# Gates table of a product-key layer: first keys made by GpSimd with their weights, state split moved one stage earlier

## The chip, the core and the metric

The kernel runs on one core of one Trainium2 chip. The core has five engines with queues of their own: TensorE (PE in the profile; PEld is its weight load), VectorE (DVE), ScalarE (ACT), GpSimd (POOL) and SyncE (SP, which here only starts transfers). The metric is the device time of one execution in microseconds, less is better. The median of three runs before the change is 2322.55 us.

## What is computed

The reference is one step of a streaming encoder layer for 512 prompt tokens and 8 x 16 sample tokens (640 tokens, 1024 features): stick-breaking and latent attention, then a product-key layer. Only the latter matters here. For each token, 8 heads choose 16 of 128 x 128 experts each:

```python
q = (x @ w_peer_q).reshape(n, PEER_HEADS, 2, PEER_HALF)
s1 = jnp.einsum('nhk,ek->nhe', q[:, :, 0], sub_keys_1)
s2 = jnp.einsum('nhk,ek->nhe', q[:, :, 1], sub_keys_2)
...
gate = jax.nn.softmax(top_s, axis=-1)
...
act = jax.nn.gelu(jnp.einsum('td,thkd->thk', xt, u), approximate=False) * gt
return jnp.einsum('thk,thkd->td', act, v_experts[it])
```

So a token's result is a sum over its 128 chosen experts (8 heads x 16) of gate x gelu(token . u) x v. The expert's number is first key x 128 + second key.

## The kernel before, in words

The kernel is written by hand as eight phases, one after the other, each a block of one instruction queue per engine that ends with a barrier of all engines; semaphores order the work inside a block. The 640 tokens are five tiles of 128. The first two tiles (GT = 2) get their experts by gathering rows from memory; the other three (DN = 384 tokens, "dense") run against all 16,384 experts, with a table of gates that is zero where an expert was not chosen. The last three phases matter.

**phase_keys** (line 1583) makes queries and scores on TensorE, ScalarE copies them out of PSUM (queries at L1664, scores at L1676), and VectorE finds the 16 best per head (MAX8, FIND_INDEX8 and MATCH_REPLACE8, which read one tensor). After a tile's maxima VectorE casts the indices (L1777), adds candidates (L1780 to L1784), finds the best pairs, and compares (L1812). GpSimd then multiplies and adds up these comparisons for tiles 0 to 3 (L1637, L1641, L1650), VectorE those of tile 4 (L1815 on). The results for the dense tokens are transposed into `sel`: for every dense token, a column of 128 first keys, 128 second keys and 128 gates, one per partition.

**phase_gates** (line 1868) builds the table of gates. For each token, `first` holds on each of 128 partitions (one per head and choice) a row of 128 zeros with the gate at the chosen first key, `second` a row with a one at the chosen second key; TensorE multiplies the two and so sums the 128 choices into a 128 x 128 table. The work goes in groups of G = 4 tokens, 96 groups in all, with four buffers of `first` and `second` and four PSUM banks in turn. Before the change VectorE makes the first keys of three tokens in one comparison without weights (L1949), those of the fourth with the weight in one tensor_scalar of two operations (L1953), and all four second keys (L1954). ScalarE multiplies the three unweighted ones by their gates (`weigh`, L1990) and copies a finished bank into `stage` (L1997). TensorE waits for `hot_ready` (VectorE), `weighed` (ScalarE) and a free bank (`table_ready`), and signals `hot_used`, for which VectorE waits four groups later. SP stores every 64 tokens of the table to memory (L1927, the last ones in four parts, L1931). GpSimd has other work at the start: it splits the dense tokens' normed state `hT` into a rounded upper part `h[0]` (cast, L1936) and the rest `h[1]` (subtraction, L1938), which the experts phase multiplies by; then it issues the first three gathers of expert rows (AHEAD = 3, L1864, in `gather`). SP loads the first `vraw` tiles after the split, since they lie over `hT`.

**phase_experts** (line 2004) runs 128 chunks of 128 experts: TensorE transposes `u` (L2189), multiplies in split precision (L2200, L2212); ScalarE and VectorE copy and split (L2124, L2239, L2163, L2290); GpSimd multiplies by the gates (L2117) and issues the gathers; VectorE works on the gathered rows (L2249, L2263).

Of the kernel before, what the change touches and what calls it, by code (L numbers as in the profile page):

```python
# [25 lines left out]
F32R = mybir.dt.float32r  # L26
ALU = mybir.AluOpType
ACT = mybir.ActivationFunctionType
# [3 lines left out]
P = 128  # L32
D = 1024
KD = D // P
# [5 lines left out]
N = SEQ + NSEQ * STEP  # L40
NT = N // P
PT = SEQ // P
HALF = N // 2
GT = 2
DT = NT - GT
DN = DT * P
# [11 lines left out]
NKEYS = 128  # L58
TOPK = 16
NEXP = NKEYS * NKEYS  # L60
NQ = 2 * H
# [11 lines left out]
HI, LO = 0, 1  # L73
# [719 lines left out]
def phase_prompt_attention(nc, A, env):  # L793
# [19 lines left out]
             "mT_psum aT_psum mT0 mT1 aT0 aT1 om_psum os_psum om_out os_out").split()  # L813
    S = {n: sem("pa_" + n) for n in names}
    ROUNDS = [(i, hp) for i in range(PT) for hp in range(H // 2)]
# [767 lines left out]
def phase_keys(nc, A, env):  # L1583

    sb, sem, PS, C, ident = (env[k] for k in ("sb", "sem", "PS", "C", "ident"))
    hT = env["hT"]
# [20 lines left out]
    sel = sb("sel", 10, [P, 3, DN])  # L1607
    eidx = sb("eidx", 14.5, [P, GT, H * TOPK], U32)
    egate = sb("egate", 15.5, [P, GT, H * TOPK])
    htok = sb("htok", 122, [P, GT, D])  # L1610
# [2 lines left out]
    place, work = sb("place", 148, [P, H * TOPK]), sb("work", 148.5, [P, 2, H * TOPK])  # L1613
    flat_stat = env["stat"][:].rearrange("p a b -> p (a b)")
    total, peak = flat_stat[:, 0:NT * H], flat_stat[:, 64:64 + H]
    env["env"].update(sel=sel, eidx=eidx, egate=egate, htok=htok)
    names = "sk_psum sk_ready q_ready s_psum s_ready topped ranked gate_exp gates sel_psum sel_ready0 sel_ready1 h_psum h_turned hot_ready hot_used picking picked step".split()
    S = {n: sem("pk_" + n) for n in names}
    S["q_psum"] = env["q_psum"]
    skey_raw = env["skey_raw"]  # L1620
# [1 line left out]
    with nc.Block() as block:  # L1622
# [4 lines left out]
        @block.gpsimd  # L1627
        def _(pool):
            step = Step(pool, S["picking"])

            def sync(ins):
                step(ins)
                step.wait()

            for t in range(NT - 1):
                pool.wait_ge(S["hot_ready"], t + 1)
                sync(pool.tensor_tensor(hot[:], hot[:], topf[t % 2][:].unsqueeze(3).broadcast_to((P, NQ, TOPK, TOPK)), ALU.mult))  # L1637
                src = hot
                for half in halves:
                    w = half.shape[2]  # L1640
                    ins = pool.tensor_tensor(half[:], src[:, :, 0:w, :], src[:, :, w:2 * w, :], ALU.add)  # L1641
                    if src is hot:
                        ins.then_inc(S["hot_used"], 1)
                        pool.wait_ge(S["hot_used"], t + 1)
                    else:
                        sync(ins)
                    src = half
                pairs = src[:].rearrange("p (h i) m k -> p h i m k", i=2)
                for i in range(2):
                    ins = pool.tensor_tensor(pick[:, t, i, :].rearrange("p (h k) -> p h k", h=H), pairs[:, :, i, 0, :], pairs[:, :, i, 1, :], ALU.add)  # L1650
                    if i == 0:
                        step(ins)
                ins.then_inc(S["picked"], 1)

        @block.scalar
        def _(act):
# [211 lines left out]
def phase_gates(nc, A, env):  # L1868

    sb, sem, PS, C, sel = (env[k] for k in ("sb", "sem", "PS", "C", "sel"))  # L1870
    hT = env["hT"]
    stage = [sb(f"stage{i}", 138 + 32 * i, [P, NKEYS, TB]) for i in range(2)]
    G = 4
    first = [sb(f"first{i}", 66 + 2 * i, [P, G, NKEYS]) for i in range(G)]
    second = [sb(f"second{i}", 74 + 2 * i, [P, G, NKEYS]) for i in range(G)]

    h = [sb("h_hi", 82, [P, KD, DN], F32R), sb("h_lo", 94, [P, KD, DN], F32R)]
    dense = hT[:, :, GT * P:N]
    u = [sb(f"u{i}", 106 + 4 * i, [P, D]) for i in range(4)]
    vraw = [sb(f"vraw{i}", 46 + 4 * i, [P, D]) for i in range(2)]  # L1880
    rows = [sb(f"rows{i}", at, [P, D]) for i, at in enumerate((54, 58, 62, 10, 203, 176, 180, 184, 188, 192, 196))]
    v_in = [nc.alloc_semaphore(f"v_in{i}") for i in range(2)]
    row_in = [nc.alloc_semaphore(f"row_in{i}") for i in range(len(rows))]
    parts = [nc.alloc_semaphore(f"gates_part{i}") for i in range(PARTS)]
    steps = gather_order()
    eidx = env["eidx"]
    env["env"].update(h=h, u=u, vraw=vraw, rows=rows, v_in=v_in, row_in=row_in, steps=steps, gates_parts=parts)
    h_split, u_in = sem("gt_h_split"), sem("gt_u_in")
    S = {n: sem("gt_" + n) for n in "marked hot_ready weighed hot_used table_ready".split()}

    stored = [nc.alloc_semaphore(f"gates_stored{i}") for i in range(2)]
    env["env"].update(gates_stored=stored)
# [24 lines left out]
    with nc.Block() as block:  # L1917
        @block.sync
        def _(sp):
            for i in range(len(u)):  # L1920
                sp.dma_start(u[i][:], A["u_experts"][0, i * P:(i + 1) * P, :]).then_inc(u_in, 16)
            sp.wait_ge(h_split, 2)
            for i in range(2):
                sp.dma_start(vraw[i][:], A["v_experts"][0, i * P:(i + 1) * P, :]).then_inc(v_in[i], 16)
            for b in range(BLOCKS - 1):
                sp.wait_ge(S["table_ready"], (b + 1) * PB + G)
                sp.dma_start(A["gates"][b], stage[b % 2][:]).then_inc(stored[b % 2], 16)  # L1927
            sp.wait_ge(S["table_ready"], BLOCKS * PB + G)
            for i in range(PARTS):
                keys = slice(i * NKEYS // PARTS, (i + 1) * NKEYS // PARTS)  # L1930
                sp.dma_start(A["gates"][BLOCKS - 1, :, keys, :], stage[1][:, keys, :]).then_inc(parts[i], 16)  # L1931
            sp.wait_ge(u_in, 16 * len(u))

        @block.gpsimd
        def _(pool):
            pool.tensor_copy(h[0][:], dense).then_inc(h_split, 1)  # L1936
            pool.wait_ge(h_split, 1)
            pool.tensor_tensor(h[1][:], dense, h[0][:], ALU.subtract).then_inc(h_split, 1)  # L1938
            pool.wait_ge(h_split, 2)
            for n in range(AHEAD):  # L1940
                gather(pool, A, eidx, steps, rows, row_in, n)

        @block.vector
        def _(dve):
            def body(n, g, e, at, token, last):

                dve.wait_ge(S["hot_used"], n + 1)

                dve.tensor_tensor(first[g][:, 0:G - 1, :], C["iota"].unsqueeze(1).broadcast_to((P, G - 1, NKEYS)),  # L1949
                                  sel[:, 0, bass.ds(token, G - 1)].unsqueeze(2).broadcast_to((P, G - 1, NKEYS)), ALU.is_equal  # L1950
                                  ).then_inc(S["marked"], 1)
                col = bass.ds(token + (G - 1), 1)
                dve.tensor_scalar(first[g][:, G - 1, :], C["iota"], sel[:, 0, col], sel[:, 2, col], ALU.is_equal, ALU.mult)  # L1953
                dve.tensor_tensor(second[g][:], C["iota"].unsqueeze(1).broadcast_to((P, G, NKEYS)),  # L1954
                                  sel[:, 1, bass.ds(token, G)].unsqueeze(2).broadcast_to((P, G, NKEYS)), ALU.is_equal
                                  ).then_inc(S["hot_ready"], 1)

            loop(dve, body)

        @block.tensor  # L1960
        def _(pe):

            pe.sem_inc(S["hot_used"], G)

            def body(n, g, e, at, token, last):
                pe.wait_ge(S["hot_ready"], n + 1)
                pe.wait_ge(S["weighed"], n + 1)
                pe.wait_ge(S["table_ready"], n + 1)
                for j in range(G):
                    mm = pe.matmul(PS[:, g, j * NKEYS:(j + 1) * NKEYS], second[g][:, j, :], first[g][:, j, :], start=True, stop=True)  # L1970
                mm.then_inc(S["hot_used"], 1)

            loop(pe, body)

        @block.scalar
        def _(act):

            act.sem_inc(S["table_ready"], G)
            for e in range(2):
                act.sem_inc(stored[e], 16)  # L1980

            def edge(pair, e):

                act.wait_ge(stored[e], pair * 16 + 16)

            def weigh(n, g, token):

                act.wait_ge(S["marked"], n + 1)
                for j in range(G - 1):
                    ins = act.activation(first[g][:, j, :], first[g][:, j, :], ACT.Copy, scale=sel[:, 2, bass.ds(token + j, 1)])  # L1990
                ins.then_inc(S["weighed"], 1)

            def body(n, g, e, at, token, last):
                if not last:
                    weigh(n + 1, (g + 1) % G, token + G)
                act.wait_ge(S["hot_used"], n + G + 1)
                act.activation(stage[e][:, :, bass.ds(at, G)], PS[:, g, :].rearrange("p (n i) -> p i n", n=G),  # L1997
                               ACT.Copy).then_inc(S["table_ready"], 1)

            weigh(0, 0, 0)  # L2000
            loop(act, body, edge)


# [334 lines left out]
```

## Time and profile before

| | before |
|---|---|
| median of 3 runs (2321.29 to 2323.34) | 2322.55 us |
| the profiled execution's own time | 2334.51 us |
| its span, first to last instruction | 2332.2 us |
| mean granted TensorE clock | 0.964 |
| TensorE busy | 2102.0 us, 90% |
| VectorE busy | 1607.0 us, 69% |
| ScalarE busy | 817.0 us, 35% |
| GpSimd busy | 939.2 us, 40% |
| transfers | 537.66 MB, mean 231 GB/s |

The shares are averages over stages that differ. The span divides at the barriers; the keys stage ends at about 961 us, the gates stage at 1115, and the experts stage takes the rest. An instruction's time in a row is its record from start to end. On VectorE and ScalarE the next instruction of the same queue may start before the last one's record ends, so the distance between starts says what an instruction costs when the engine is full.

### The profile page before, as it was taken

Reading aid. Unit: us, or ns where it says so; the run is one execution under the profiler, and the core shown is the slowest. Engines: PE = TensorE matmul, PEld = TensorE weight load, DVE = VectorE, ACT = ScalarE, POOL = GpSimd, SP = SyncE. Lnnn points to the kernel's source line nnn. Section 1 sums busy time; section 2 is a strip of 40 time slices with the busy share of each in tenths; the row PEclk is TensorE's granted clock in tenths of the full one; section 3 lists DMA queues with packets and bytes.
Section 4 is the critical chain, followed back from the end, with each engine's and each line's share of the span. In section 5 each row is a group of like instructions: output and inputs, shape, how many; then the busy total and the mean of one; then the engine's idle time right before and its main releaser. Section 6 shows DMA issues by size and latency. Waiting matters only on the chain.

```text
span 2332.2 us, 34960 instructions
## 1 busy us (share of the span) xinstructions
PE 2102.0 (90%) x12419; PEld 1834.2 (79%) x12419; DVE 1607.0 (69%) x3194; ACT 817.0 (35%) x1534; POOL 939.2 (40%) x732
## 2 busy tenths in 40 slices
PE   6997888688999997377699999999999999999997
PEld 6895577566665997266688999998998898999996
DVE  1423255434324799999577888888888888888887
ACT  2313245322233111399233333333333333333333
POOL 0001011100000145200576767666766766777773
PEclk9998799999999998699899999999999999999998
DMA  6311132243260000244999999999999999999995
GB/s 235 124 41 54 55 127 73 65 151 120 87 264 1 1 2 1 81 189 171 341 339 359 343 373 361 359 369 350 373 353 366 361 360 365 355 377 355 365 368 186
DMA packets 193925, 537.66 MB, mean 231 GB/s; under 512 B 19845, under 2 KB 76458, under 8 KB 191658
## 3 DMA queue, kind: packets, MB, share of 16 engines
q1 hardware_dynamic: 119808, 267.53, 32.2%
q0 software_dynamic: 73728, 268.47, 30.2%
q8 instruction: 44, 0.72, 0.1%
q10 hardware_dynamic: 298, 0.55, 0.1%
q14 instruction: 47, 0.39, 0.1%
HBM read 505.35 MB, written 31.15 MB: 230 GB/s over the span
## 4 chain that ended last, share of the span: by engine, by line
PE 43%; DVE 6%; DMA 6%; issue 2%; DVEq 1%; SPq 0%; ACT 0%; POOL 0%; POOLq 0%
PE PS L2200 19%; PE PS L2212 19%; DMA u<-in_u_experts 5%; PE PS L2189 4%; DVE second L1954 2%; DVE first L1953 1%; DVE first L1949 1%; DVE rows L2249 1%; PE PS L1970 1%; DVE v_l L2290 0%; DMA gates<-stage 0%; DVE vacc L2263 0%; POOL rows L1864 0%; ACT uT_h L2124 0%; DVEq L1954 0%
## 5 line engine op out<-in xcount | busy, mean ns | idle before, releaser
L1864 POOL DMA_INDIRECT rows<-in_v_experts,eidx x256 | 423.1, 1653 | 76.8 <-issue 70.5
L1864 POOL DMA_INDIRECT rows<-in_u_experts,eidx x256 | 273.5, 1068 | 206.7 <-POOLq L160 140.2
L2200 PE MATMUL PS<-h_hi,uT_h 128*128 128x384 f32 x1024 | 355.9, 348 | 0.0
L2200 PE MATMUL PS<-h_hi,uT_l 128*128 128x384 f32 x1024 | 345.4, 337 | 0.0
L2200 PE MATMUL PS<-h_lo,uT_h 128*128 128x384 f32 x1024 | 344.6, 336 | 0.0
L2263 DVE SCALAR_TENSOR_TENSOR vacc<-rows,egate,vacc 128x1024 f32<-128x1024 f32 x254 | 329.6, 1298 | 2.2
L2239 DVE TENSOR_TENSOR uT_l<-PS,uT_h 128x512 fp32r<-128x512 f32 x256 | 177.0, 692 | 205.9 <-ACT uT_h L2124 205.9
L2249 DVE SCALAR_TENSOR_TENSOR rows<-rows,htok 128x1024 f32<-128x1024 f32 x256 | 312.2, 1224 | 0.0
L2212 PE MATMUL PS<-v_h,a_h 128*128 128x512 f32 x768 | 310.8, 405 | 0.0
L2212 PE MATMUL PS<-v_l,a_h 128*128 128x512 f32 x768 | 300.0, 391 | 0.0
L2124 ACT ACTIVATE uT_h<-PS 128x512 fp32r<-128x512 f32 x256 | 153.4, 599 | 365.0 <-PE PS L2189 364.8
L2212 PE MATMUL PS<-v_h,a_l 128*128 128x512 f32 x768 | 238.1, 391 | 0.0
L2117 POOL TENSOR_TENSOR gl<-gl,gt 128x384 f32<-128x384 f32 x128 | 134.7, 1052 | 225.5 <-ACT gl L2168 225.4
L2200 PEld LDWEIGHTS PS<-h_lo,uT_h 128*128 128x128 f32 x1024 | 194.3, 190 | 0.0
L2200 PEld LDWEIGHTS PS<-h_hi,uT_h 128*128 128x128 f32 x1024 | 194.2, 190 | 0.0
L2200 PEld LDWEIGHTS PS<-h_hi,uT_l 128*128 128x128 f32 x1024 | 193.8, 189 | 0.0
L2168 ACT ACTIVATE gl<-PS 128x384 f32<-128x384 f32 x128 | 63.0, 492 | 334.7 <-PE PS L2200 334.7
L2189 PE MATMUL PS<-const,u 128*128 128x128 f32 x1024 | 156.2, 275 | 23.1 <-DMA u<-in_u_experts 11.7
L2212 PEld LDWEIGHTS PS<-v_h,a_l 128*128 128x128 f32 x768 | 144.2, 188 | 31.4
L2189 PEld LDWEIGHTS PS<-const,u 128*128 128x128 f32 x1024 | 126.7, 141 | 49.3 <-issue 15.8
L2212 PEld LDWEIGHTS PS<-v_l,a_h 128*128 128x128 f32 x768 | 144.7, 188 | 26.0
L2212 PEld LDWEIGHTS PS<-v_h,a_h 128*128 128x128 f32 x768 | 144.4, 188 | 26.1
(350 smaller groups left out, 3567.1 us busy)
## 6 DMA issues: line engine op xcount, KB each, us to landing
u<-in_u_experts SPq DMA_DIRECT2D x128, 512.0 KB, 7.5
vraw<-in_v_experts SPq DMA_DIRECT2D x128, 512.0 KB, 6.3
gt<-gates SPq DMA_DIRECT2D x32, 768.0 KB, 9.5
gates<-stage SPq DMA_DIRECT2D x5, 4096.0 KB, 11.5
wada_b<-in_w_ada SPq DMA_DIRECT2D x16, 1024.0 KB, 5.2
wada<-in_w_ada SPq DMA_DIRECT2D x8, 1024.0 KB, 12.0
kc<-in_cache_sb_k SPq DMA_DIRECT2D x8, 1024.0 KB, 7.6
vc<-in_cache_sb_v SPq DMA_DIRECT2D x8, 1024.0 KB, 5.6
```

The lines of the kernel that those rows point to most:

```text
L1864: pool.indirect_dma_start(out=rows[slot][:], out_offset=None, in_=A["u_experts" if kind == "u" else "v_experts"][0], in_offset=bass.Indire ...
L1949: dve.tensor_tensor(first[g][:, 0:G - 1, :], C["iota"].unsqueeze(1).broadcast_to((P, G - 1, NKEYS)), sel[:, 0, bass.ds(token, G - 1)].unsq ...
L1954: dve.tensor_tensor(second[g][:], C["iota"].unsqueeze(1).broadcast_to((P, G, NKEYS)), sel[:, 1, bass.ds(token, G)].unsqueeze(2).broadcast_ ...
L2117: pool.tensor_tensor(act_by_block, act_by_block, gt[e][:, :, c, :], ALU.mult).then_inc(S["weighed"], 1)
L2124: act.activation(uT[q % 2][HI][:, 4 * b:4 * b + 4, :], PS[:, 0, :].rearrange("p (k n) -> p k n", k=4), ACT.Copy).then_inc(S["uT_hi"], 1)
L2168: act.activation(gl[q % 2][:], PS[:, 1, 0:DN], ACT.Gelu).then_inc(S["gelu"], 1)
L2189: mm = pe.transpose(PS[:, 0, j * P:(j + 1) * P], u[q % UR][:, k * P:(k + 1) * P], ident)
L2200: mm = pe.matmul(PS[:, 1, 0:DN], uT[q % 2][w][:, k, :], h[m][:, k, :], start=k == 0 and (w, m) == PASSES[0], stop=k == KD - 1 and (w, m) = ...
L2212: mm = pe.matmul(PS[:, 2 + 2 * t + b, :], a[q % 2][w][:, t * P:(t + 1) * P], v[q % 2][m][:, b * 512:(b + 1) * 512], start=fresh and (w, m) ...
L2239: dve.tensor_tensor(uT[q % 2][LO][:, 4 * b:4 * b + 4, :], PS[:, 0, :].rearrange("p (k n) -> p k n", k=4), uT[q % 2][HI][:, 4 * b:4 * b + 4 ...
L2249: dve.scalar_tensor_tensor(out=row[:], in0=row[:], scalar=1.0, in1=htok[:, t, :], op0=ALU.mult, op1=ALU.mult, accum_out=dots[:, t, j:j + 1 ...
L2263: dve.scalar_tensor_tensor(out=vacc[:, t, :], in0=row[:], scalar=egate[:, t, j:j + 1], in1=vacc[:, t, :], op0=ALU.mult, op1=ALU.add).then_ ...
```

## The change

GpSimd makes the first keys of the first three tokens of each group of four, each by one tensor_scalar over 128 elements that compares with the key and multiplies by the gate (96 x 3 instructions, written out and not looped). VectorE keeps the fourth token's first key and the second keys. ScalarE keeps only the copy out of PSUM, and the semaphore `weighed` is gone; TensorE waits for `marked`, now GpSimd's, instead. GpSimd's instructions wait for `hot_used` as VectorE's do. The split of `hT` into `h` moves from the start of phase_gates to the end of GpSimd's queue in phase_keys, behind a wait for the last queries; SP's wait for the split in front of its `vraw` loads is gone. The three gathers stay in phase_gates and come after GpSimd's 288 instructions.

```diff
--- before.py
+++ after.py
@@ -1613,8 +1613,9 @@
     place, work = sb("place", 148, [P, H * TOPK]), sb("work", 148.5, [P, 2, H * TOPK])
     flat_stat = env["stat"][:].rearrange("p a b -> p (a b)")
     total, peak = flat_stat[:, 0:NT * H], flat_stat[:, 64:64 + H]
-    env["env"].update(sel=sel, eidx=eidx, egate=egate, htok=htok)
-    names = "sk_psum sk_ready q_ready s_psum s_ready topped ranked gate_exp gates sel_psum sel_ready0 sel_ready1 h_psum h_turned hot_ready hot_used picking picked step".split()
+    h = [sb("h_hi", 82, [P, KD, DN], F32R), sb("h_lo", 94, [P, KD, DN], F32R)]
+    env["env"].update(sel=sel, eidx=eidx, egate=egate, htok=htok, h=h)
+    names = "sk_psum sk_ready q_ready s_psum s_ready topped ranked gate_exp gates sel_psum sel_ready0 sel_ready1 h_psum h_turned hot_ready hot_used picking picked h_split step".split()
     S = {n: sem("pk_" + n) for n in names}
     S["q_psum"] = env["q_psum"]
     skey_raw = env["skey_raw"]
@@ -1651,6 +1652,13 @@
                     if i == 0:
                         step(ins)
                 ins.then_inc(S["picked"], 1)
+
+            pool.wait_ge(S["q_psum"], NT * (NQ // 4))
+            dense = hT[:, :, GT * P:N]
+            pool.tensor_copy(h[HI][:], dense).then_inc(S["h_split"], 1)
+            pool.wait_ge(S["h_split"], 1)
+            pool.tensor_tensor(h[LO][:], dense, h[HI][:], ALU.subtract).then_inc(S["h_split"], 1)
+            pool.wait_ge(S["h_split"], 2)
 
         @block.scalar
         def _(act):
@@ -1874,8 +1882,6 @@
     first = [sb(f"first{i}", 66 + 2 * i, [P, G, NKEYS]) for i in range(G)]
     second = [sb(f"second{i}", 74 + 2 * i, [P, G, NKEYS]) for i in range(G)]
 
-    h = [sb("h_hi", 82, [P, KD, DN], F32R), sb("h_lo", 94, [P, KD, DN], F32R)]
-    dense = hT[:, :, GT * P:N]
     u = [sb(f"u{i}", 106 + 4 * i, [P, D]) for i in range(4)]
     vraw = [sb(f"vraw{i}", 46 + 4 * i, [P, D]) for i in range(2)]
     rows = [sb(f"rows{i}", at, [P, D]) for i, at in enumerate((54, 58, 62, 10, 203, 176, 180, 184, 188, 192, 196))]
@@ -1884,9 +1890,9 @@
     parts = [nc.alloc_semaphore(f"gates_part{i}") for i in range(PARTS)]
     steps = gather_order()
     eidx = env["eidx"]
-    env["env"].update(h=h, u=u, vraw=vraw, rows=rows, v_in=v_in, row_in=row_in, steps=steps, gates_parts=parts)
-    h_split, u_in = sem("gt_h_split"), sem("gt_u_in")
-    S = {n: sem("gt_" + n) for n in "marked hot_ready weighed hot_used table_ready".split()}
+    env["env"].update(u=u, vraw=vraw, rows=rows, v_in=v_in, row_in=row_in, steps=steps, gates_parts=parts)
+    u_in = sem("gt_u_in")
+    S = {n: sem("gt_" + n) for n in "marked hot_ready hot_used table_ready".split()}
 
     stored = [nc.alloc_semaphore(f"gates_stored{i}") for i in range(2)]
     env["env"].update(gates_stored=stored)
@@ -1919,7 +1925,6 @@
         def _(sp):
             for i in range(len(u)):
                 sp.dma_start(u[i][:], A["u_experts"][0, i * P:(i + 1) * P, :]).then_inc(u_in, 16)
-            sp.wait_ge(h_split, 2)
             for i in range(2):
                 sp.dma_start(vraw[i][:], A["v_experts"][0, i * P:(i + 1) * P, :]).then_inc(v_in[i], 16)
             for b in range(BLOCKS - 1):
@@ -1933,10 +1938,13 @@
 
         @block.gpsimd
         def _(pool):
-            pool.tensor_copy(h[0][:], dense).then_inc(h_split, 1)
-            pool.wait_ge(h_split, 1)
-            pool.tensor_tensor(h[1][:], dense, h[0][:], ALU.subtract).then_inc(h_split, 1)
-            pool.wait_ge(h_split, 2)
+            for n in range(DN // G):
+                pool.wait_ge(S["hot_used"], n + 1)
+                for j in range(G - 1):
+                    col = slice(n * G + j, n * G + j + 1)
+                    ins = pool.tensor_scalar(first[n % G][:, j, :], C["iota"], sel[:, 0, col], sel[:, 2, col], ALU.is_equal, ALU.mult)
+                ins.then_inc(S["marked"], 1)
+
             for n in range(AHEAD):
                 gather(pool, A, eidx, steps, rows, row_in, n)
 
@@ -1946,9 +1954,6 @@
 
                 dve.wait_ge(S["hot_used"], n + 1)
 
-                dve.tensor_tensor(first[g][:, 0:G - 1, :], C["iota"].unsqueeze(1).broadcast_to((P, G - 1, NKEYS)),
-                                  sel[:, 0, bass.ds(token, G - 1)].unsqueeze(2).broadcast_to((P, G - 1, NKEYS)), ALU.is_equal
-                                  ).then_inc(S["marked"], 1)
                 col = bass.ds(token + (G - 1), 1)
                 dve.tensor_scalar(first[g][:, G - 1, :], C["iota"], sel[:, 0, col], sel[:, 2, col], ALU.is_equal, ALU.mult)
                 dve.tensor_tensor(second[g][:], C["iota"].unsqueeze(1).broadcast_to((P, G, NKEYS)),
@@ -1964,7 +1969,7 @@
 
             def body(n, g, e, at, token, last):
                 pe.wait_ge(S["hot_ready"], n + 1)
-                pe.wait_ge(S["weighed"], n + 1)
+                pe.wait_ge(S["marked"], n + 1)
                 pe.wait_ge(S["table_ready"], n + 1)
                 for j in range(G):
                     mm = pe.matmul(PS[:, g, j * NKEYS:(j + 1) * NKEYS], second[g][:, j, :], first[g][:, j, :], start=True, stop=True)
@@ -1983,21 +1988,11 @@
 
                 act.wait_ge(stored[e], pair * 16 + 16)
 
-            def weigh(n, g, token):
-
-                act.wait_ge(S["marked"], n + 1)
-                for j in range(G - 1):
-                    ins = act.activation(first[g][:, j, :], first[g][:, j, :], ACT.Copy, scale=sel[:, 2, bass.ds(token + j, 1)])
-                ins.then_inc(S["weighed"], 1)
-
             def body(n, g, e, at, token, last):
-                if not last:
-                    weigh(n + 1, (g + 1) % G, token + G)
                 act.wait_ge(S["hot_used"], n + G + 1)
                 act.activation(stage[e][:, :, bass.ds(at, G)], PS[:, g, :].rearrange("p (n i) -> p i n", n=G),
                                ACT.Copy).then_inc(S["table_ready"], 1)
 
-            weigh(0, 0, 0)
             loop(act, body, edge)
 
 
```

## Rows read from the trace of the kernel before

**Rows 1.** Stages: us, then busy us (x instructions) by engine, PEclk, DMA share, GB/s.
```profile
885.00:961.00 76.00, 34.25 (x292) 32.91 (x290) 72.30 (x393) 9.35 (x15) 24.33 (x12) 0.73 0.00 1
...
971.50:1111.00 139.50, 109.92 (x768) 94.48 (x768) 131.58 (x285) 136.82 (x381) 3.28 (x3) 0.99 0.40 169
...
1125.00:2310.00 1185.00, 1169.49 (x6345) 1061.81 (x6345) 987.26 (x1291) 400.24 (x656) 824.66 (x635) 1.00 0.96 357
```

**Rows 2.** Timeline of one steady group; columns: start us, us, engine, line, operation.
```profile
1097.81 0.56 DVE L1949 TENSOR_TENSOR first<-const,sel 128x384 f32<-128x384 f32 x1
1097.81 0.58 ACT L1997 ACTIVATE stage<-PS 128x512 f32 x1
...
1098.29 0.34 DVE L1953 TENSOR_SCALAR first<-const,sel 128x128 f32<-128x128 f32 x1
1098.29 0.97 ACT L1990 ACTIVATE first<-first,sel 128x128 f32<-128x128 f32 x3
1098.54 0.68 DVE L1954 TENSOR_TENSOR second<-const,sel 128x512 f32<-128x512 f32 x1
...
1099.28 0.56 DVE L1949 TENSOR_TENSOR first<-const,sel 128x384 f32<-128x384 f32 x1
```

**Rows 3.** Timeline of the start of the gates stage.
```profile
961.10 2.75 POOL L1936 CAST h_hi<-hT 128x3072 fp32r<-128x3072 f32 x1 [32.29 <-POOLq L160]
961.76 2.50 DVE L1949 TENSOR_TENSOR first<-const,sel 128x384 f32<-128x384 f32 x1 [1.47 <-PEq L1963]
963.93 6.84 POOL L1938 TENSOR_TENSOR h_lo<-hT,h_hi 128x3072 fp32r<-128x3072 f32 x1
964.18 6.67 DVE L1953 TENSOR_SCALAR first<-const,sel 128x128 f32<-128x128 f32 x1
...
971.06 1.42 POOL L1864 DMA_INDIRECT rows<-in_u_experts,eidx  x1 [0.29 <-POOL h_lo L1938]
...
971.51 4.91 PE L1970 MATMUL PS<-first,second 128*128 128x128 f32 x24 [11.82 <-DVE second L1954]
...
974.37 1.02 POOL L1864 DMA_INDIRECT rows<-in_u_experts,eidx  x1 [0.31 <-issue]
```

**Rows 4.** GpSimd groups by shape: count, busy us, mean ns, idle before.
```profile
L622 POOL COPY qz<-qT 64x2048 f32<-64x2048 f32 x2 | 3.8, 1887 | 0.1
...
L1650 POOL TENSOR_TENSOR pick<-halves 128x128 f32<-128x128 bf16 x8 | 3.2, 425 | 0.3
```

**Rows 5.** Timeline of the experts stage, two places.
```profile
1499.33 1.02 POOL L2117 TENSOR_TENSOR gl<-gl,gt 128x384 f32<-128x384 f32 x1 [3.05 <-ACT gl L2168]
...
1507.57 1.21 DVE L2290 TENSOR_TENSOR v_l<-vraw,v_h 128x1024 fp32r<-128x1024 f32 x1
...
1508.51 1.15 POOL L2117 TENSOR_TENSOR gl<-gl,gt 128x384 f32<-128x384 f32 x1 [2.32 <-ACT gl L2168]
```

**Rows 6.** Timeline of the keys stage, from its fifth tile on.
```profile
912.98 0.60 ACT L1664 ACTIVATE qp<-PS 128x512 f32<-128x512 f32 x1 [6.55 <-PE PS L1707]
...
928.00 0.81 POOL L1650 TENSOR_TENSOR pick<-halves 128x128 f32<-128x128 bf16 x2
...
933.53 0.29 DVE L1777 CAST topf<-topi 128x256 bf16<-128x256 uint32 x1
933.74 0.28 DVE L1780 TENSOR_TENSOR cand<-top 128x128 f32<-128x128 f32 x1
```

**Rows 7.** Timeline of the end of the gates stage.
```profile
1109.22 1.13 PE L1970 MATMUL PS<-first,second 128*128 128x128 f32 x8 [0.24 <-issue]
...
1111.01 3.07 SPq L1931 DMA_DIRECT2D gates<-stage  x4
...
1115.02 0.90 PE L2189 MATMUL PS<-const,u 128*128 128x128 f32 x4 [4.66 <-PEq L160]
```

**Rows 8.** Tile rows, 960 to 1120 us: its gathers, issue to landing.
```profile
DMA to landing us min/median/max: 5.8/7.9/11.3
```

**Rows 9.** Chain of waits into the experts stage: start us, us, what.
```profile
1112.83 11.37 DMA gates<-stage
```

## The prediction

> **What bounds the kernel now.** I read the stage table first. The gates table takes 139.5 us, the experts stage some 1185 us, and what the change edits lies in the first, at its two ends, and in the last microseconds of the keys stage [rows 1]. In the gates stage ScalarE is busy 136.8 of 139.5 us and VectorE 131.6, TensorE 109.9, GpSimd 3.3: the two elementwise engines set the pace, GpSimd is free. The timeline of one group shows how: ScalarE weighs three keys (0.97 us) and evicts (0.58 to 0.60), VectorE starts its three instructions 0.48, 0.25 and 0.74 us apart, 1.47 us in all, and starts the next three-token comparison in the moment in which ScalarE begins an eviction [rows 2]. TensorE's groups start from 971.51 to 1109.22 us, 96 of them: 137.71 / 95 = **1.45 us a group** [rows 3, 7]. TensorE needs 1.13 us for one [rows 7].
>
> The stage also begins late. VectorE's first comparison of 384 elements takes 2.50 us instead of 0.56, its first tensor_scalar 6.67 instead of 0.34; the first ends 0.4 us after GpSimd's cast, the second 0.1 us after GpSimd's subtraction, and the first matmul comes only at 971.51 [rows 2, 3]. GpSimd never computes beside VectorE in the rest of the stage, so this start is the one place that tells what the new arrangement does all along: **the two engines take turns**. The ends tell how: 964.26 less the usual 0.55 is 963.71, 0.14 before the cast's end; 970.85 less 0.34 is 970.51, 0.26 before the subtraction's end. I take 0.19: VectorE gets through about 0.19 us before GpSimd's record ends. The other way round, GpSimd's product of 384 elements in the experts stage, 1.02 us beside a VectorE operation that reads PSUM, takes 1.15 when it starts 0.27 us before the end of a VectorE subtraction with two inputs in SBUF, so it gets through 0.14 us before that record ends [rows 4, 5].
>
> **The change, part by part.**
>
> *Removed from ScalarE:* three weighings a group, 0.97 us; it keeps 0.60 and bounds nothing. *Removed from VectorE:* the 384-element comparison, 0.48 us of spacing; it keeps 0.25 and 0.60 (0.68 less the 0.08 by which the next one overlaps, as 0.56 stands 0.48 apart), some 0.85 us. Both alone would let TensorE's 1.13 us set the pace.
>
> *Added to GpSimd:* 288 tensor_scalars of 128 elements with two operations and two scalars a partition. The trace has none on GpSimd. From below: a one-input copy of 2048 elements takes 1.887 us, a cast of 3072 takes 2.745 [rows 3, 4]; that is 0.84 ns an element, so 128 elements take 1.887 - 1920 x 0.00084 = 0.28 us, if second operation and scalars are free. From above: a 128-element product of two inputs takes 0.425 [rows 4]; twice that, were each operation a pass of its own, 0.85. I take 0.35, halfway between the one-input and the two-input row: it has one tensor to read but more to compute than a copy.
>
> *The pace with turns.* With c for one GpSimd instruction: VectorE's two instructions of a group each slip in between two of GpSimd's. Such a gap costs GpSimd c - 0.19 + VectorE's hold (0.68 - 0.14 = 0.54 for the second keys; for the tensor_scalar, whose 0.34 is partly queue, its spacing of 0.25 - 0.14 = 0.11); the third costs c less the 0.04 by which GpSimd's neighbours overlap (0.81 for two of 0.425 [rows 6]). Sum: 3c - 0.38 + 0.65 - 0.04 = **3c + 0.23**. At 0.35 it is 1.28, above TensorE's 1.13, so 95 x (1.28 - 1.45) = **-16.2 us**. At 0.28 it is 1.07 and TensorE's 1.13 decides: -30.4. At 0.425 it is 1.505: +5.2. At 0.85 it is 2.78: +126. Four buffers let each engine run ahead, so no wait of one group adds to the next; ScalarE's wait for the keys is replaced by TensorE's own.
>
> *The split leaves the stage's start.* Its 2.75 and 6.84 us no longer hold VectorE. The first GpSimd key can start at 961.1, three take 1.1, VectorE's first pair slips in: first matmul at about 963.3 instead of 971.5: **-8.2 us** [rows 3].
>
> *It arrives in the keys stage.* GpSimd's last sum there ends at 928.81; the new wait is for the last queries, whose matmuls are done by then (ScalarE's last copy of them starts at 912.98), and nothing is queued behind. So cast from 928.9 to 931.6, subtraction from 931.7 to **938.6**. VectorE meanwhile runs maxima with one input, which do not collide, but at 933.53 comes a cast and at 933.74 an addition with two inputs in SBUF [rows 6]. By the behaviour above they wait until 938.4. VectorE is busy 72.3 of these 76 us [rows 1] and nothing absorbs it: 938.4 - 933.5 = **+4.9 us**, or 0 if only GpSimd's share of time suffers. I take it whole, since the same subtraction held VectorE once already.
>
> The Trainium skill's page SBUF — State Buffer, section Who interferes with whom, says that VectorE and GpSimd share one pair of ports as an exclusive lock, held for the whole instruction, when VectorE has two SBUF inputs or a two-port mode. The 6.67 us tensor_scalar agrees. Perfetto Trace Analysis, section Optimizing Scalar/DVE Operations, draws from it that moving work between these two engines might not help; by it the ports' sum above is the pace, and without it TensorE's 1.13 would be.
>
> *SP:* the two vraw loads lose their wait and start some 9 us earlier, beside nothing; 0. *The three gathers* move behind GpSimd's 288 instructions. From the first's start to the third's is 3.31 us [rows 3], and gathers land 5.8 us after issue at best [rows 8]. If the stage's end waits for the landing, GpSimd is done 0.3 + 3.31 + 5.8 = 9.4 us after its last key, against 4.9 us for the last matmul, the eviction and SP's four stores (1109.22 to 1114.1) [rows 7]: +4.5; if it waits for their issue only, 0. The experts stage's first product waits anyway for the last store's landing, 11.37 us after 1112.83 [rows 9], which hides a part. I take **+2**.
>
> **Sum:** -16.2 - 8.2 + 4.9 + 2 = -17.5. The profiled execution took 2334.51 us around a span of 2332.2, 12 us over the median of 2322.55; the stages' differences should carry over. 2322.55 - 17.5 = **2305.0**. The experts stage, 1185 us with TensorE 1169 busy and the transfers at 0.96, starts earlier and is otherwise unmoved.
>
> **Rivals.** (A) *GpSimd is slow enough to be the bound.* Place: its queue, three keys a group. Above a pace of 1.45 + (8.2 - 4.9 - 2)/95 = 1.46, that is c = 0.41, the change costs time. At c = 0.50: 95 x (1.73 - 1.45) - 1.3 = +25, 2348; at 0.85, 2447. For it: two operations, a comparison and two scalars from SBUF in an instruction of only 128 elements, where fixed cost weighs most. Against: one tensor input. (B) *GpSimd is as quick as a copy, or the engines overlap:* TensorE's 1.13 sets the pace, -30.4 - 1.3 = -32, 2291; with no collision in keys either, 2286. Against it: the 2.50 and 6.67 us of VectorE. (C) *The parts cancel:* c between 0.395 and 0.425, within 5 us of 2322.55.
>
> The GPSIMD Engine Reference, section Engine selection, calls one-input work on GpSimd roughly line-rate; by that page rival (B) is what happens, with the copy's 0.28 as its nearest row here.
>
> **Chances.** The forecast (c from 0.31 to 0.395) 0.31, (B) 0.17, (C) 0.13, (A) 0.39. (A) is large because the bounds reach much further above 0.41 than below, and only the choice of halfway between the two nearest rows puts mine below. 0.2% is 4.6 us, about what a measurement of this kernel can tell from no change. Faster 0.48, same 0.13, slower 0.39. The range leaves out the far tail of (A) above c = 0.54 (+37) and little of (B): 2284 to 2360. The forecast's own range is 2294 to 2318.
>
> **What would show it.** A GpSimd group L1944 or so, x288, with its mean: 0.35 means right, above 0.41 (A). VectorE's tensor_scalar and second keys longer than 0.34 and 0.68 on average show the turns; as short as now with a pace of 1.13, (B). First matmul about 2 us into the stage. VectorE's cast of the fifth tile's indices in the keys stage some 5 us long instead of 0.29. A gap between the end of the stores' issue (1114.1) and the first transpose (1115.02) above the present 0.9 us [rows 7] would be the gathers. ScalarE idle more than half of the stage. I am wrong if the stage from first to last group takes over 139 us, or if the experts stage changes its length by more than 5 us.

## The result and the profile after

The changed kernel takes **2452.05 us** (median of 4 runs, 2446.94 to 2458.50) against 2321.92 us before: ratio 1.054, 95% interval 1.051 to 1.056. The forecast was 2305, the range ended at 2360.

The profiled execution took 2446.94 us around a span of 2445.2, 5 us under its median, where that of before was 12.6 over the 2321.92 us, the median of four runs. So the spans differ by 113.0 us and the medians by 130.1; no trace places the 17 us between the two. (Later runs of the kernel before, beside the experiments, have medians of some 2329 us; against them the difference is 123.) The page of the changed kernel, its span and two groups (count, busy us, mean ns, idle before):

```profile
span 2445.2 us, 34453 instructions
...
L1945 POOL TENSOR_SCALAR first<-const,sel 128x128 f32<-128x128 f32 x288 | 261.3, 920 | 27.6 <-PEq L1968 27.6
...
L1975 PE MATMUL PS<-first,second 128*128 128x128 f32 x768 | 192.9, 431 | 72.1 <-issue 61.5
```

GpSimd's new instruction takes 0.92 us on average, where 0.35 was forecast. Its stage table (columns as in [rows 1]):

```profile
885.00:964.50 79.50, 33.16 (x282) 31.82 (x280) 75.74 (x384) 9.36 (x15) 32.66 (x13) 0.72 0.00 1
968.10:1226.10 258.00, 190.87 (x760) 166.18 (x760) 89.32 (x187) 56.32 (x95) 257.94 (x285) 0.52 0.21 91
...
1228.00:1240.00 12.00, 0.19 (x1) 0.01 (x1) 0.00 (x0) 0.60 (x1) 1.56 (x2) 0.50 0.99 379
```

GpSimd is busy 257.9 of 258.0 us; VectorE and ScalarE, which bounded the stage before, are idle for most of it. TensorE's granted clock is 0.52 there, the 1.2 GHz level, where it was 0.99 in the kernel before; a group of its matmuls then takes 2.05 us, which still fits into the pace. All instructions that touch `first` and `second` in the changed kernel (duration ns min/median/max):

```profile
L1945 POOL TENSOR_SCALAR first<-const,sel x288: 783/787/1412, 964.8 to 1225.3; 128x128 f32<-128x128 f32 x144
L1958 DVE TENSOR_SCALAR first<-const,sel x96: 332/347/500, 965.4 to 1218.2; 128x128 f32<-128x128 f32 x96
...
L1959 DVE TENSOR_TENSOR second<-const,sel x96: 677/684/858, 965.6 to 1218.5; 128x512 f32<-128x512 f32 x96
```

The second and third GpSimd key of a group have a median of 0.786 us, the first one of 1.13, up to 1.41, while VectorE's medians are as before. Waits in the stage from 968 to 1226 us (us in total, times, longest):

```profile
ACT stage L1993 <- PE PS L1975: 207.0, 95, 7.5
DVE first L1958 <- PE PS L1975: 161.6, 92, 3.2
```

Both follow TensorE. The profile puts most of TensorE's own idle time (61.3 us) down to no engine; that it waits for GpSimd is concluded from GpSimd having no gap in these 258 us, and experiment 4 bears it out. The ends of the stage, in the changed kernel's timeline (answers to [rows 3], [rows 6] and [rows 7]):

```profile
930.48 6.65 POOL L1660 TENSOR_TENSOR h_lo<-hT,h_hi 128x3072 fp32r<-128x3072 f32 x1
932.44 4.85 DVE L1785 CAST topf<-topi 128x256 bf16<-128x256 uint32 x1
937.20 0.28 DVE L1788 TENSOR_TENSOR cand<-top 128x128 f32<-128x128 f32 x1
...
963.18 0.56 DVE L1847 COPY sel<-PS 128x384 f32<-128x384 f32 x1 [1.00 <-PE PS L1747]
...
968.07 2.04 PE L1975 MATMUL PS<-first,second 128*128 128x128 f32 x8 [4.92 <-POOL first L1945]
...
1226.14 2.05 PE L1975 MATMUL PS<-first,second 128*128 128x128 f32 x8 [0.27 <-issue]
...
1228.93 0.94 POOL L1872 DMA_INDIRECT rows<-in_u_experts,eidx  x1 [0.30 <-issue]
...
1240.02 1.08 PE L2184 MATMUL PS<-const,u 128*128 128x128 f32 x4 [11.83 <-PEq L160]
```

From these starts the 113.0 us divide without a rest:

| stretch | before | changed | difference |
|---|---|---|---|
| up to VectorE's cast for the fifth tile | 933.53 | 932.44 | -1.1 |
| from there to the end of the last copy into `sel` | 26.8 | 31.3 | +4.5 |
| to the first matmul of the gates stage | 11.2 | 4.3 | -6.9 |
| to the last group's first matmul | 137.7 | 258.1 | **+120.4** |
| to the experts' first transpose | 5.8 | 13.9 | +8.1 |
| experts, to the end | 1217.2 | 1205.1 | -12.0 |

The pace of a group is 258.07 / 95 = 2.72 us instead of 1.45.

### The profile page after: what moved, and what is told of

Read it like the earlier page. It is cut to its first block and busy times, and to the rows that moved or that the text cites. A ratio compares the mean times of both kernels' runs of the same rounds, so it can differ in the third digit from the quotient of the medians.

```text
span 2445.2 us, 34453 instructions
## 1 busy us (share of the span) xinstructions
PE 2180.2 (89%) x12419; PEld 1903.4 (78%) x12419; DVE 1561.3 (64%) x3098; ACT 736.3 (30%) x1246; POOL 1201.2 (49%) x1020
## 5 line engine op out<-in xcount | busy, mean ns | idle before, releaser
L1945 POOL TENSOR_SCALAR first<-const,sel 128x128 f32<-128x128 f32 x288 | 261.3, 920 | 27.6 <-PEq L1968 27.6
L1975 PE MATMUL PS<-first,second 128*128 128x128 f32 x768 | 192.9, 431 | 72.1 <-issue 61.5
L1975 PEld LDWEIGHTS PS<-first,second 128*128 128x128 f32 x768 | 168.0, 322 | 97.1 <-issue 85.7
```

The source lines that it names most:

```text
L1945: ins = pool.tensor_scalar(first[n % G][:, j, :], C["iota"], sel[:, 0, col], sel[:, 2, col], ALU.is_equal, ALU.mult)
```

## Experiments

Paces below are, as above, from the first matmul of the first group to that of the last, divided by 95. Each ratio is to runs of the kernel before on the same chip, whose medians lay between 2328.9 and 2329.2 us. The forecast times start from the 2321.92 us above, so they are some 7 us low beside the medians below.

**1. The split alone** (`split_only`). The kernel before, with the two halves of the split at the end of GpSimd's queue in the keys stage:

```diff
+            pool.wait_ge(S["q_psum"], NT * (NQ // 4))
+            dense = hT[:, :, GT * P:N]
+            pool.tensor_copy(h[HI][:], dense).then_inc(S["h_split"], 1)
+            pool.wait_ge(S["h_split"], 1)
+            pool.tensor_tensor(h[LO][:], dense, h[HI][:], ALU.subtract).then_inc(S["h_split"], 1)
+            pool.wait_ge(S["h_split"], 2)
```

As in the change, SP's wait for the split goes with it.

> The split alone moves to the keys stage; keys are made as before. Theory 1 (the GpSimd keys alone are the loss; the split's move is small): the cast of the fifth tile's indices waits some 4.8 us as in the changed kernel, the first matmul of the gates stage comes 7 to 8 us sooner after the stage begins, and the kernel is 2 to 5 us faster than before, 2317 to 2320. Theory 2 (the moved split costs as much as it gives, or its collision in the keys stage spreads): within 2 us of before or slower.

Measured: ratio 0.9981 (0.9961 to 1.0002), some 4 us faster, at the edge of what can be told. In its timeline:

```profile
924.04 6.65 POOL L1660 TENSOR_TENSOR h_lo<-hT,h_hi 128x3072 fp32r<-128x3072 f32 x1
926.00 4.83 DVE L1785 CAST topf<-topi 128x256 bf16<-128x256 uint32 x1
```

The cast waits 4.5 us. From the last copy into `sel` to the first matmul it is 3.15 us instead of 11.22, so 8.1 us come back. The pace is 1.45, untouched. The sum, 8.1 - 4.5 = 3.6, agrees with theory 1; the interval of the times alone would not exclude theory 2.

**2. The keys alone** (`keys_only`). The changed kernel, with the split back ahead of GpSimd's keys.

> GpSimd makes the keys, the split stays at the start of the gates stage. Theory 1: the whole loss is here: a pace of 2.7 us a group against 1.45, +120 us for 95 groups, first matmul some 12 us after the stage's start since GpSimd's first keys stand behind the split, so 2450 to 2465, 3 to 10 us above the changed kernel. Theory 2 (the two parts of the change only lose together): under 2400.

Measured: ratio 1.0527 (1.0495 to 1.0559), median 2451.44; pace 2.71; 14.1 us from the last copy to the first matmul. Its VectorE instruction on the fourth key shows the old collision as its maximum:

```profile
L1957 DVE TENSOR_SCALAR first<-const,sel x96: 335/346/6667, 956.4 to 1218.8; 128x128 f32<-128x128 f32 x96
```

The whole loss is in the keys. That it is 3 to 10 us slower than the changed kernel did not come out: the ratios' intervals overlap.

**3. What a GpSimd instruction costs by itself** (`forms`). A block ahead of the gates stage, all other engines idle:

```diff
+            four(lambda i: pool.tensor_scalar(out[:, i, 0:128], src[:, 0:128], key, gate, ALU.is_equal, ALU.mult))
+            four(lambda i: pool.tensor_scalar(out[:, i, 0:128], src[:, 0:128], key, gate, ALU.mult, ALU.mult))
+            four(lambda i: pool.tensor_scalar(out[:, i, 0:128], src[:, 0:128], key, None, ALU.is_equal))
...
```

> A block of GpSimd instructions in fours, with all other engines idle, stands ahead of the gates stage; the rest is the kernel before, so the total is longer by some 50 us. Theory 1 (the instruction itself is long): tensor_scalar of 128 elements with is_equal and mult and two scalars per partition costs 0.77 us from start to start with nobody beside it; 256 elements tell the part per element. If the cost is per element and operation, 512 elements take 2.2 us or more and the one-operation form is shorter by a third or more; if it is a fixed cost per instruction, 512 elements take about 1.1 us. Theory 2 (it is short and only VectorE's turns stretch it): 0.3 to 0.45 us for 128 elements.

Its GpSimd groups, each line of the kernel one form (columns as in [rows 4]); L1892 to L1895 are is_equal and mult with two scalars per partition, L1896 and L1897 mult and mult with the same, L1898 and L1899 is_equal alone, L1902 and L1903 mult alone by a constant written into the instruction, L1904 a copy:

```profile
L1895 POOL TENSOR_SCALAR bench<-x,sel 128x1024 f32<-128x1024 f32 x4 | 15.1, 3777 | 0.1
L1894 POOL TENSOR_SCALAR bench<-x,sel 128x512 f32<-128x512 f32 x4 | 8.2, 2071 | 0.1
...
L1899 POOL TENSOR_SCALAR bench<-x,sel 128x512 f32<-128x512 f32 x4 | 6.2, 1560 | 0.1
L1903 POOL TENSOR_SCALAR bench<-x 128x512 f32<-128x512 f32 x4 | 5.8, 1488 | 0.1
...
L1892 POOL TENSOR_SCALAR bench<-x,sel 128x128 f32<-128x128 f32 x4 | 3.1, 788 | 32.4 <-PEq L1875 32.4
L1897 POOL TENSOR_SCALAR bench<-x,sel 128x512 f32<-128x512 f32 x4 | 3.0, 768 | 0.1
...
L1898 POOL TENSOR_SCALAR bench<-x,sel 128x128 f32<-128x128 f32 x4 | 2.3, 601 | 0.1
...
L1902 POOL TENSOR_SCALAR bench<-x 128x128 f32<-128x128 f32 x4 | 2.0, 530 | 0.1
L1896 POOL TENSOR_SCALAR bench<-x,sel 128x128 f32<-128x128 f32 x4 | 1.7, 447 | 0.1
...
L1904 POOL COPY bench<-x 128x128 f32<-128x128 f32 x4 | 1.0, 293 | 0.1
```

The changed kernel's instruction takes 0.788 us with nobody beside it. The slopes split it: (3.777 - 0.788) / 896 = **3.34 ns an element** for is_equal and mult, (1.560 - 0.601) / 384 = 2.50 for is_equal alone, (0.768 - 0.447) / 384 = **0.84** for mult and mult, as much as a copy. So at 128 elements 0.36 us are fixed and 0.43 go with the elements. The comparison is dear, not the second operation as such, nor the scalars. The copy's 0.293 confirms the lower bound of the prediction (0.28).

The expectation's own signs came out in between. 512 elements take 2.07 us, neither the 2.2 or more of a cost per element and operation nor the 1.1 of a fixed cost, and the form with the comparison alone is shorter by a quarter (0.601 against 0.788, 1.560 against 2.071) and not by a third: there is a fixed part and a part per element. The kernel with the block takes 2410.58 us in its one run, some 81 more than before, not 50.

**4. No comparison; comparison alone** (`mults_only`, `compare_only`). In the changed kernel:

```diff
-sel[:, 0, col], sel[:, 2, col], ALU.is_equal, ALU.mult)
+sel[:, 0, col], sel[:, 2, col], ALU.mult, ALU.mult)
```

and, in the other, `sel[:, 0, col], None, ALU.is_equal)`.

> The changed kernel with is_equal replaced by mult in GpSimd's first keys, so the table holds other numbers; nothing else moves. Theory 1 (the comparison makes the instruction long): from the forms block, 0.43 us from start to start, so three plus some 0.4 for turns with VectorE: 1.6 to 1.75 us a group, the kernel 2330 to 2350 against 2452. If the formula of the prediction holds at this c (0.446 as a record), 3c + 0.23 = 1.57. Rival (turns with VectorE or the two scalars set the pace): 2.3 us a group or more.

> The changed kernel with the second operation left out of GpSimd's first keys, so the gates are missing in three of four keys. Theory 1: 0.58 us from start to start as in the forms block, plus 0.4 for turns: 2.1 to 2.2 us a group, the kernel 2390 to 2400. Rival (a fixed cost per instruction, whatever it computes): 2.7 as in the changed kernel.

`mults_only` first, then `compare_only`, each from its answer on `first`:

```profile
L1945 POOL TENSOR_SCALAR first<-const,sel x288: 440/443/1023, 960.1 to 1132.5; 128x128 f32<-128x128 f32 x144
```

```profile
L1945 POOL TENSOR_SCALAR first<-const,sel x288: 592/597/1200, 964.5 to 1168.7; 128x128 f32<-128x128 f32 x144
```

Paces of 1.80 and 2.13 us, times of 2358.78 and 2392.98 us, one run each. The pace follows the instruction, and GpSimd is busy without a gap in both stages (165.0 of 165.0 us and 195.0 of 195.0), while TensorE's granted clock is 0.99 in the first and 0.79 in the second: neither a fixed cost nor that clock sets the pace. The comparison alone came out as forecast. With mult and mult the pace missed its 1.6 to 1.75 by a little, and the time its 2330 to 2350: over three spacings of 0.43 there are 0.51 us for turns, over three of 0.58 and of 0.773 only 0.39 and 0.40. Why turns cost more there is open. Even at the price of two multiplications the change would have been slower than before (1.80 against 1.45 us a group).

**5. The turns taken away** (`psum_ruler`). The changed kernel, with VectorE's row of 0 to 127 copied once into a free PSUM bank:

```diff
+            dve.tensor_copy(PS[:, 4, 0:NKEYS], C["iota"]).then_inc(S["ruler"], 1)
...
-                dve.tensor_tensor(second[g][:], C["iota"].unsqueeze(1)
+                dve.tensor_tensor(second[g][:], ruler.unsqueeze(1)
```

and the same in the tensor_scalar of the fourth key.

> The changed kernel, but VectorE reads the row 0 to 127 from a bank of PSUM, so its two instructions a group have one input in SBUF at most. Theory (turns are taken over the second way into SBUF): all 288 GpSimd instructions take 0.79 us, none is stretched, the pace falls from 2.72 to 3 x 0.773 = 2.32 to 2.36 us, the kernel is 34 to 38 us faster than the changed one, 2413 to 2418. Rival (one GpSimd instruction in three is long because of its wait for TensorE or for another reason): the stretched ones stay and the pace is 2.6 or more.

Measured: ratio 1.0326 (1.0277 to 1.0374), median 2408.09; pace **2.326**. The stage is 37.1 us shorter than in the changed kernel, the profiled span 37.8. GpSimd's timeline at one place:

```profile
1049.39 7.17 POOL L1945 TENSOR_SCALAR first<-const,sel 128x128 f32<-128x128 f32 x9
```

The pace came out as forecast. The median is 5 us below its range and, by the ratios, some 50 us below the changed kernel's; what goes beyond the stage's 37 no trace places. Another detail did not come out either: GpSimd's records are not all 0.79 us but have a median of 1.03. Their starts, though, stand less than 0.8 us apart in 286 of 287 cases; in the changed kernel in 178. A GpSimd record can be long while its engine loses nothing; the distance between starts is what counts. The 0.39 us a group that went is the price of the turns, about a third of the loss per group (0.39 of 1.27). Both of VectorE's instructions were moved at once, so how it divides between them is not shown.

**6. The gathers first** (`gathers_first`). The changed kernel, with the loop over the three gathers ahead of the keys' loop.

> The changed kernel with the three gathers ahead of GpSimd's keys. Theory (the stage's end waits until the gathers' rows have landed beside the table's last stores): from the last group's first matmul to the experts' first transpose 6 to 7 us instead of 13.9, the first matmul of the stage 3 to 4 us later since the keys stand behind the gathers, and the experts stage some 8 us longer again, for it waits for the last store instead. In sum within 5 us of the changed kernel. Rival (the 13.9 us come from TensorE's halved clock or the stores): it stays above 12.

Its timeline at the stage's end:

```profile
1225.36 1.13 PE L1974 MATMUL PS<-first,second 128*128 128x128 f32 x8 [0.67 <-issue]
...
1227.15 3.07 SPq L1936 DMA_DIRECT2D gates<-stage  x4
1231.15 1.09 PE L2183 MATMUL PS<-const,u 128*128 128x128 f32 x4 [4.66 <-PEq L160]
```

The end shrinks from 13.9 to 5.8 us, the experts stage grows from 1205.1 to 1214.8, and the first matmul comes 4.2 us later. Ratio 1.0487 (1.0433 to 1.0541), median 2443.93, an interval that overlaps the changed kernel's; the profiled spans are 2446.0 and 2445.2 us. So the block's end does wait for the gathers to land. In the changed kernel the last one lands at 1239.1 us, 10.2 after its issue and 0.9 before the experts' first transpose. The wait itself costs nothing here: end and experts stage together take 1217 to 1224 us in the five traces with late gathers and 1219 to 1225 in the seven with early ones (1219.0 changed, 1223.0 before, 1220.6 here).

**7. The split where it collides with nothing** (`split_tucked`). The first experiment, with one wait more for the subtraction, counted by VectorE's last addition of candidates:

```diff
+            pool.wait_ge(S["cands"], NT)
             pool.tensor_tensor(h[LO][:], dense, h[HI][:], ALU.subtract).then_inc(S["h_split"], 1)
```

> As the split alone, but its subtraction waits until VectorE has made the fifth tile's candidates, so that it runs beside maxima with one input. Theory 1 (turns are taken only with two-input or two-port VectorE work): the cast of the indices takes about 0.3 to 0.5 us again, nothing else of VectorE gets longer, the subtraction ends before 943 us, and the kernel is 7 to 9 us faster than before, 2313 to 2316. Rival (any work of GpSimd that reads SBUF slows VectorE): no faster than the split alone, within 1 us of it.

Its timeline:

```profile
928.22 0.29 DVE L1786 CAST topf<-topi 128x256 bf16<-128x256 uint32 x1
...
929.16 0.22 DVE L1793 TENSOR_TENSOR cand<-top 128x64 f32<-128x64 f32 x1
929.53 6.67 POOL L1661 TENSOR_TENSOR h_lo<-hT,h_hi 128x3072 fp32r<-128x3072 f32 x1 [3.36 <-DVE cand L1793]
```

From the cast to the last copy it is 26.8 us as before, and the 8.1 us at the start of the gates stage are kept. Ratio 0.9953 (0.9934 to 0.9972), median 2318.54: **faster by 11 us**, the forecast's 7 to 9 inside the interval (6.5 to 15.4). VectorE's maxima and index searches, one SBUF input each, run beside a long GpSimd subtraction at no cost. One SBUF input is not the whole condition, though: the cast of experiment 1 has one too, and it waited.

**8. One key of four on GpSimd** (`one_of_four`, then `one_of_four_psum`). ScalarE weighs two keys instead of three, VectorE compares two tokens, GpSimd makes the third's fused, VectorE the fourth's. In both kernels the three gathers also stand ahead of GpSimd's keys, as in experiment 6, which the expectations do not say:

```diff
+                pool.tensor_scalar(first[n % G][:, 2, :], C["iota"], sel[:, 0, col], sel[:, 2, col], ALU.is_equal, ALU.mult).then_inc(S["fused"], 1)
...
-                for j in range(G - 1):
+                for j in range(G - 2):
                     ins = act.activation(first[g][:, j, :], ...
```

> The split alone moved, and GpSimd makes only the third token's first key of each four; VectorE compares two tokens without weights and makes the fourth's, ScalarE weighs two. By rows of the other runs: ScalarE 2 x 0.33 + 0.60 = 1.26 us a group, GpSimd 0.77, VectorE 0.35 + 0.25 + 0.60 = 1.2 and its turns with GpSimd. Theory (turns take VectorE 0.79 - 0.19 = 0.6 us for each GpSimd instruction that it meets): 1.6 to 1.8 us a group, worse than the 1.45 of before, the kernel 15 to 35 us slower than before less 4 for the split. Rival (so little GpSimd work hides in VectorE's gaps): 1.26 to 1.35 us, 10 to 18 us faster from it.

> The same division of the keys, with VectorE's row read from PSUM and the split behind the candidates. Theory: no turns are taken, so ScalarE's 1.26 and VectorE's 0.35 + 0.31 + 0.60 = 1.26 set the pace: 1.27 to 1.33 us a group, 11 to 17 us less in the stage, and with the split's 7 to 11 us the kernel is 18 to 28 us faster than before. Rival (reading PSUM beside TensorE's writes and ScalarE's copies costs VectorE as much as the turns did): 1.45 or more.

`one_of_four`, groups from 970 to 1080 us:

```profile
L1946 POOL TENSOR_SCALAR first<-const,sel 128x128 f32<-128x128 f32 x86 | 96.8, 1126 | 12.6 <-PE PS L1976 11.6
...
L1959 DVE TENSOR_TENSOR second<-const,sel 128x512 f32<-128x512 f32 x83 | 56.3, 679 | 0.0
```

`one_of_four_psum`, the same stretch:

```profile
L1949 POOL TENSOR_SCALAR first<-const,sel 128x128 f32<-128x128 f32 x86 | 68.3, 794 | 43.1 <-PE PS L1983 43.1
...
L1966 DVE TENSOR_TENSOR second<-PS,sel 128x512 f32<-128x512 f32 x85 | 57.9, 681 | 0.0
```

Both paces are 1.30 us. Ratios: 0.9939 (0.9918 to 0.9960), median 2316.11, and **0.9915 (0.9891 to 0.9940), median 2307.33**, both faster than the kernel before. My theory of the first was wrong, and its rival's pace right: the turns stretch GpSimd's instruction to 1.13 us on average and leave VectorE's second keys as they are (0.68 us), since GpSimd's fits in the pace either way. The second came out as forecast, but PSUM brought nothing to the pace here; in the traces the two differ mainly in where the split stands (31.3 and 26.8 us from VectorE's cast to the last copy into `sel`). The early gathers cost both something: the first matmul comes 7.5 and 6.5 us after that copy, where it was 3.1 in experiment 1.

## Why the prediction was wrong

**The step that failed** is the price of GpSimd's instruction: "I take 0.35, halfway between the one-input and the two-input row". It is 0.787 us. The rows that I put it between were a copy and a product, and neither compares; on this engine, in the block of experiment 3, the comparison alone takes 2.50 ns an element against 0.84 for two multiplications. It is a term mis-sized by 2.2 times, and as it is paid three times a group on the engine that bounds, all else is small beside it. The stage was forecast 16.2 us shorter and is 120.4 longer: of these 136.6 us, 3 x 0.437 x 95 = 124.5 are the price, and 12 the turns' constant below. My upper end, 0.85, held, and rival (A) at 0.85 gave 2447 us, 5 below what was measured. That is partly luck: at the real 0.787 the same sum gives 2430, and a c too high made up for a constant too small. The range was cut at c = 0.54, although no row excluded a larger c. That was the second mistake: it should have reached to the bound that I had worked out.

**The pace with turns**, 3c + 0.23, gives 2.59 at 0.787 where 2.72 was measured, 2.02 against 2.13 at 0.597, and 1.56 against 1.80 at 0.443. That the pace rises by three times the price and that turns come on top is right (experiments 4 and 5); its constant is 0.11 to 0.24 too small, most where the instruction is short. So the gain would have failed at c = 0.35 too: with the 0.47 that the run with two multiplications shows in place of 0.23, my estimate is 3 x 0.35 + 0.47 = 1.52 us a group, above the 1.45 of before. The sign named for the turns hardly showed either: VectorE's two records grew to means of 0.367 and 0.696 us only, and the turns stood in GpSimd's.

**The split:** -8.2 at the start of the gates stage was forecast; experiment 1 shows -8.1, and -6.9 with GpSimd's slower keys. +4.9 in the keys stage was forecast, +4.5 measured, at the very instruction named. The earlier `vraw` loads change nothing that a run here singles out.

**The gathers:** "+2" for the stage's end. The end became 8.1 us longer, more than the +4.5 given as the most, since the last landing took 10.2 us beside the stores and not 5.8. But the experts stage gave it back, -12.0 us, more than the 5 that the prediction allowed it. Experiment 6 shows the exchange, and so do all traces: the experts stage takes 1203.4 to 1208.5 us with late gathers, 1213.3 to 1218.7 with early ones. A part has the reason that the prediction names: before, GpSimd's first product stood behind the last store's landing, 18.5 us after the first transpose, and now it comes after 13.2. Where the other 6 to 7 us come from is open.

**The rivals:** (A) is what happened, with a chance of 0.39, the largest of the four. (B) fell with the price. The rule of the Trainium skill, GPSIMD Engine Reference, section Engine selection, that one-input work is roughly line-rate on GpSimd, holds here for a copy and for two multiplications by scalars from SBUF (0.84 ns an element), and not for a comparison (2.50) or for a multiplication by a constant written into the instruction ((1.488 - 0.530) / 384 = 2.49). The exclusive lock that the Trainium skill's page SBUF — State Buffer, section Who interferes with whom, describes agrees with experiment 5 (2.72 to 2.33 us a group once VectorE's row came from PSUM) and experiment 7 (26.8 us with the subtraction beside maxima, as before).

## What to carry to other kernels

Price a GpSimd elementwise instruction by its own operation: where the trace has no row of that form, a handful in an idle block tells it, and until then the range reaches to the upper bound. One short instruction in the shadow of a group's pace can pay (one key of four: 1.30 us a group against 1.45), while three on one queue made it the bound (2.72). Long GpSimd work that reads SBUF belongs beside VectorE work that a trace shows unharmed by it, here maxima and index searches: the same 9.4 us of split cost 4.5 us where a cast fell into it, and nothing beside maxima alone. A single SBUF input is no safe sign, since the cast has one.

## What the runs showed that I had not expected

GpSimd multiplies faster by two scalars from SBUF (0.768 us for 512 elements, two operations) than by one constant written into the instruction (1.488 us, one operation). And the length of a GpSimd record is no measure of its cost: with VectorE's row in PSUM the records grew to a median of 1.03 us while their starts had a median distance of 0.77.
